# Two slabs of a modulation matrix-vector product taken later in a one-core transformer kernel's weight stream

## The reference

```python
c_act = jax.nn.silu(c)
ada = c_act @ w_ada[l] + b_ada[l]
sh_m, sc_m, g_m, sh_f, sc_f, g_f = jnp.split(ada, N_ADA, axis=-1)
h = modulate(rmsnorm(x, norm_mix_g[l]), sh_m, sc_m)
mix = hybrid_mixer(h, ...)              # MLA heads and forgetting heads, gated
x = x + g_m[:, None, :] * mix
h = modulate(rmsnorm(x, norm_ffn_g[l]), sh_f, sc_f)
x = x + g_f[:, None, :] * conv_ffn(h, ...)
```

## Time and profile before

| | us |
|---|---|
| median of 3 runs | 1008.37 |
| lowest and highest | 1008.07, 1008.6 |
| the profiled execution | 1008.82 |
| its span on the core | 1007.0 |
| PE busy in the span | 997.8 |
| DVE busy | 703.0 |
| ACT busy | 590.5 |

### The profile page before, as it was taken

One profiled execution on the slowest core, in us unless ns is written; L12 is line 12 of the kernel. 1 busy time (PEld: TensorE's weight loads), 2 busy tenths in 40 slices (PEclk: granted clock), 3 DMA queues, 4 the chain that ended last, 5 costly groups with the idle time before them and its releaser, 6 DMA issues.

```text
span 1007.0 us, 17093 instructions
## 1 busy us (share of the span) xinstructions
PE 997.8 (99%) x6928; PEld 911.0 (90%) x6928; DVE 703.0 (70%) x1179; ACT 590.5 (59%) x987; POOL 0.4 (0%) x5
## 2 busy tenths in 40 slices
PE   9999999999999999999999999999999999999997
PEld 7899999999999999999999888888999899888886
DVE  4698888878888777787658665655766558565552
ACT  4778665647555556767647445554666547555453
POOL 0000000000000000000000000000000000000000
PEclk9999999999999999999999999999999999999999
DMA  9865668545667545563326555555553326545521
GB/s 382 344 248 201 244 229 302 192 164 209 216 255 261 193 169 178 196 210 126 127 85 220 203 205 201 175 180 201 215 189 136 127 105 251 200 176 177 203 81 42
DMA packets 28013, 196.76 MB, mean 195 GB/s; under 512 B 3104, under 2 KB 3744, under 8 KB 4640
## 3 DMA queue, kind: packets, MB, share of 16 engines
q1 hardware_dynamic: 27360, 194.95, 53.6%
q10 hardware_dynamic: 576, 0.72, 0.2%
HBM read 194.61 MB, written 1.05 MB: 194 GB/s over the span
## 4 chain that ended last, share of the span: by engine, by line
PE 97%; DVE 1%; ACT 1%; DMA 1%; issue 0%; ACTq 0%; SPq 0%
PE PS L1023 11%; PE PS L1024 11%; PE PS L1025 11%; PE PS L1207 10%; PE PS L1298 8%; PE PS L1299 8%; PE PS L1300 8%; PE PS L1210 5%; PE PS L1177 3%; PE PS L1180 3%; PE PS L1178 3%; PE PS L1240 2%; PE PS L1241 2%; PE PS L1242 2%; PE PS L1395 2%; PE PS L1384 1%
## 5 line engine op out<-in xcount | busy, mean ns | idle before, releaser
L1842 DVE TENSOR_TENSOR wlo<-raw,whi 128x1024 fp32r<-128x1024 f32 (+1 forms) x314 | 368.1, 1216 | 76.6 <-ACT whi L1460 73.9
L1460 ACT ACTIVATE whi<-raw 128x1024 fp32r<-128x1024 f32 x308 | 306.7, 1047 | 60.8 <-PE PS L1300 55.0
L1023 PE MATMUL PS<-HX,whi 128*128 128x256 f32 x816 | 234.9, 288 | 1.3 <-DVE HX L1816 1.3
L1024 PE MATMUL PS<-HX,whi 128*128 128x256 f32 x816 | 230.7, 283 | 0.0
L1025 PE MATMUL PS<-HX,wlo 128*128 128x256 f32 x816 | 230.7, 283 | 0.0
L1023 PEld LDWEIGHTS PS<-HX,whi 128*128 128x128 f32 x816 | 156.2, 191 | 7.8 <-issue 7.0
L1024 PEld LDWEIGHTS PS<-HX,whi 128*128 128x128 f32 x816 | 156.4, 192 | 0.5
L1025 PEld LDWEIGHTS PS<-HX,wlo 128*128 128x128 f32 x816 | 156.3, 192 | 0.0
L1207 PE MATMUL PS<-HX,whi 128*128 128x512 f32 x416 | 147.9, 398 | 0.0
L1298 PE MATMUL PS<-whi,Oh 128*128 128x512 f32 x344 | 134.6, 391 | 0.0
L1299 PE MATMUL PS<-wlo,Oh 128*128 128x512 f32 x344 | 134.2, 390 | 0.0
(11 more groups left out here) (262 smaller groups left out, 1599.6 us busy)
## 6 DMA issues: line engine op xcount, KB each, us to landing
raw<-wall SPq DMA_DIRECT2D x155, 1024.0 KB, 5.0
raw<-wada SPq DMA_DIRECT2D x18, 1024.0 KB, 5.0
GA<-wada SPq DMA_DIRECT2D x2, 1024.0 KB, 17.0
GA<-alibi SPq DMA_DIRECT2D x1, 2048.0 KB, 9.5
raw<-wall SPq DMA_DIRECT2D x2, 768.0 KB, 4.9
X<-xt SPq DMA_DIRECT2D x1, 1024.0 KB, 5.6
KM<-wada SPq DMA_DIRECT2D x1, 1024.0 KB, 14.5
QF<-wada SPq DMA_DIRECT2D x1, 1024.0 KB, 16.5
```

Source lines behind the costliest of these rows:

```text
L1023: e.matmul(dst, wh, a, start=start, stop=False, skip_group_check=share)
L1024: e.matmul(dst, wh, b, start=False, stop=False, skip_group_check=share)
L1460: e.activation(whi[place(n)][:, c], raw[i % RAW][:, c], ACT.Copy).then_inc(*up("a_whi", (n, half)))
L1842: e.tensor_tensor(wlo[place(n)][:, c], raw[i % RAW][:, c], f32(whi[place(n)][:, c]), ALU.subtract).then_inc(*up("v_wlo", (n, half)))
```

## The change

In the list `after` the entries 3 and 4 become 8 and 10. The first slab of part 2 (rows 0 to 255 of `w_ada`) is taken behind chunk 8 of the weights and the second behind chunk 10; the third stays behind chunk 12. Nothing is added and nothing left out, and from item 13 of the stream on each item has its old number and buffer.

```diff
     late = [("ada", cb, kk) for cb in range(2, 6) for kk in range(4)]
-    after = [3, 4, 12, 14, 15, 16, 17, 18, 19, 20, 21, 26] + [n for n in range(len(order)) if order[n][0] == "down"][1:5]
+    after = [8, 10, 12, 14, 15, 16, 17, 18, 19, 20, 21, 26] + [n for n in range(len(order)) if order[n][0] == "down"][1:5]
```

## The result

The changed kernel takes 1011.91 us in the median of five runs (1011.28 to 1012.45), against 1008.37 for the kernel before (1007.29 to 1008.6, five runs): 3.54 us more, a ratio of 1.0038 with a 95% interval of 1.0027 to 1.0048. It is slower by more than the 0.2% that can be told from no change. Two later series of the same kernel gave 1011.77 and 1012.40 against 1008.09 and 1007.86.

What follows compares the result with a forecast made beforehand. PE was taken to bound the kernel everywhere; two pauses of 1.95 and 0.95 us plus a little for restart, taken as 3.0 us, on the median of 1008.37 gave 1011.4 us, with an 8-in-10 range of 1010.2 to 1013.2.

Steps and rivals of the forecast that it cites:

- PE sets the time, and a pause is added in full: Whole kernel: PE is busy 99%, with 3.3 us of waits, so no later wait swallows a pause.
- The lateness of 3.75 us: DVE behind chunk 10, then ACT from the rope products: 1.59 + 2.51 - 0.35 = 3.75 us late.
- the lead: DVE at `apply_q` (line 1989): relief at 47 to 54 us lets it begin at 64.45, 0.39 us earlier.
- the wait used up ahead of chunk 11's split: DVE's wait of 0.35 us for ACT's split of chunk 11 takes up that much of the delay.
- The two pauses: PE waits 1.95 us for bank 2 at `ukv_values`, second half, and 0.95 us for bank 0 at chunk 12.
- The free time on DVE: DVE, 78 to 106 us: 4.64 us are free, but only 0.35 us of it ahead of the rope products.
- The second rival: DVE's free 4.64 us at 78 to 106 us swallow the 4.49 us moved in: 1008.4, not slower; chance 0.14.
- The head loop has reserve for that: in the thinnest case I found: DVE's scale ends at 146.10, PE's transposes come at 148.31: 2.2 us of reserve against 0.75 us needed.
- the third rival: PE waits once more in the head loop or for a chunk, at most 0.75 us: 1012.2; chance 0.05.
- the size on record, 3.0 us: PE's lateness after bank 0's pause: 2.90 us or slightly shorter, plus a little for restart, taken as 3.0 us.
- The clock: Rival: PE's clock falls in the pauses near 98 and 102 us, costing 1.7 us more: 1013.1; chance 0.14.
- Loads cost nothing: Slab loads issued at about 53 and 73 us, landing in 5.0 us, come in time for 73 and 88.

Runs made afterwards that it cites:

- e3: Changed kernel with the two moved slabs' instructions on 64 columns in place of 1024, all loads as in the change: 1008.37 us, ratio 1.0002.
- e4: Changed kernel with the two moved slabs' instructions on 256 columns in place of 1024, all loads as in the change: 1009.12 us, ratio 1.0011.
- e1: Kernel before with only the second slab moved, behind chunk 10; the first stays behind chunk 3: 1009.79 us, ratio 1.0018.
- e2: Kernel before with the first slab behind chunk 4 and the second behind chunk 8, none at 10: 1009.86 us, ratio 1.0019.
- e5: Changed kernel with ACT's copy of chunk 10, which frees bank 2, put ahead of the exponentials of head fox 1: 1012.50 us.
- e6: Changed kernel with the first half of part 3's sum in bank 3 instead of bank 2, so chunk 18 gets a long-free bank: 1011.59 us.
- e9: The e6 kernel run once more, against the changed kernel: 1011.07 us.
- e7: The changed kernel run once more, nothing altered, as the measure for e6: 1011.77 us.
- e8: e5 with 16 filler matmuls of 128 columns on constants put ahead of chunk 12, in its pause: 1011.58 us.

## Why the prediction was right, point by point

**PE sets the time, and a pause is added in full: right.** All that PE lost by 161 us, 3.73 us, is still there at 217 us, within 0.01, and the medians differ by 3.54.

**The lateness of 3.75 us: right, 3.72.** Its terms: slabs 1.99 and 2.51 (1.98 and 2.51 said); the lead 0.35 for 0.39 (line 1989 began at 64.49 on the old scale, 64.45 said, and waited 0.47 us for RB as said); and the wait used up ahead of chunk 11's split 0.43 for 0.35, since a row that waits for nothing also begins some 0.08 us before the one ahead of it ends (from line 2141 to the split 1.57 us before, from there to the slab 1.14 after). So 1.99 - 0.35 + 2.51 - 0.43 = 3.72: the sum on record was that near because its two small misses nearly cancel. With these two terms the same sum gives 0.21, 0.91, 1.73 and 2.16 us for e3, e4, e1 and e2, where DVE was 0.21, 0.92, 1.75 and 2.19 us late.

**The two pauses: right.** 1.96 and 0.95 us for 1.95 and 0.95. e5 shows that bank 0 alone decides their sum.

**The free time on DVE: right that it swallows nothing, with a slip.** The second rival let 4.49 us come into the stretch from 78 to 106 us. The first slab was put down at 72.47, ahead of it; only the 2.51 us of the second came in.

**"The head loop has reserve for that: in the thinnest case I found": wrong, and the term of the sum that was missed.** I had compared DVE's scale with PE's transposes, 2.2 us. The thinnest is elsewhere: chunks 17 and 18 follow each other in the same bank, because the two sums of part 3 take the two banks between. In the kernel before ACT's gate copy of chunk 17 ended at 154.14 and PE began chunk 18 at 154.20. That is no reserve at all. The copy in ACT's timeline of the kernel before:

```profile
153.57 0.57 ACT L1646 ACTIVATE GA<-PS 128x512 f32<-128x512 f32 x1
```

The same copy after; PE began chunk 18 at 157.29:

```profile
156.66 0.57 ACT L1646 ACTIVATE GA<-PS 128x512 f32<-128x512 f32 x1
```

PE's timeline of the kernel before, the transposes ahead of chunk 18 and chunk 18's first matmul:

```profile
153.22 1.04 PE L1148 MATMUL PS<-ID,ACC 128*128 128x128 f32 x8
154.20 0.39 PE L1023 MATMUL PS<-HX,whi 128*128 128x256 f32 x1
```

The last of the eight transposes began at 153.98, 0.22 us ahead of chunk 18, where in e6 the distance is 0.03: the kernel before already waited some 0.2 us there, too little for the list of waits. The 0.7 us by which ACT and DVE had fallen behind PE came out at two such places: 0.14 us at 120.92 (118.41 before), behind the two sums of part 2, and 0.57 at chunk 18. That was the third rival, priced at 0.75 us and given a chance of 0.05; with it the sum is 1008.37 + 3.75 = 1012.1 against 1011.91 measured. So the size on record, 3.0 us, was 0.5 us short of the median and 0.7 us short of the trace. Put simply, in every kernel here but e6 and e9 PE begins chunk 18 0.05 us after the end of that copy, and ends up as late as ACT was with it: 3.73 us in the changed kernel, 2.18 in e2, 1.75 in e1, 0.91 in e4, 0.20 in e3.

**The clock: right that it held behind the two pauses, but closer than the rows told.** It held there in the three profiles of the changed kernel and fell in e5, whose single pause is 2.44 us. One more run of the changed kernel (in e7, 1012.57 us) has a mean granted clock of 0.995, as the profile of e5 with its two falls; it has no profile, so where its clock fell stays open. I had also argued that the one-column matmuls at 54 us pass without a fall. They did in nine of the twelve profiles here; in e5, e7 and e9 the clock fell behind them. My other argument was the silence after PE's last matmul, during which the clock stays up for over 2 us; e5 shows that this proves little, since there it fell only when the pause was over. The price of a fall was about right: 1.7 us said, 1.45 in e5 and 1.5 at 56 us. The Trainium skill (TensorE: Matmul & The Clock Gate, "Part 1: The HAM clock gate") has a clock that is halved after idleness and given back after work; e5 and e8 agree. Idleness does not explain the falls behind the one-column matmuls: PE's timeline of e7 shows no idle time from 28 to 56 us, and the rows at 10 us, which the forecast counted for that rule, have only the 0.38 us at 8.78. No run here tells how the risk depends on the length of the pause between 1.8 and 2.4 us.

**Loads cost nothing: right,** by e3.

## What to carry to other kernels

When work is moved in the list of a busy engine, follow the lateness through every queue it feeds and compare it with the slack of each buffer that those queues free, that is, the time from its release to its next use; on an engine that never waits, the thinnest slack decides, and it may lie far behind the change, so look for it in all uses of a buffer in turn, above all where two uses of one buffer follow each other directly. The idle share of the engine that gets the work says little: only idle time that depends on nothing behind the insertion takes up a delay. And an engine that sets the time has nothing to gain from relief of another one that it doesn't wait for.

## What was not expected of the hardware

In e5 the granted clock of PE fell 1.2 us after a pause of 2.44 us had ended and cost 1.45 us, more than half of the pause again. Behind one-column matmuls it falls in some executions and not in others: between 10 and 15 us it was 0.66 in the profiles before and e1 and 1.00 in the others, and at 56 us it fell in e5, e7 and e9. No profile has both. With the start of the kernel, which differs by up to 1 us too, this puts PE 0.2 to 1.4 us earlier at 97 us in the other profiles than in that before. It is one source of the difference between single runs.
